# The prompt rows' output projection inside the decode stage, with the difference values loaded and multiplied in two halves

## Chip, cores and metric

One NeuronCore of one Trainium2 chip. The metric is the device time of one execution in microseconds (us), lower is better. The engines are TensorE (PE in the profile; PEld is its weight load), VectorE (DVE), ScalarE (ACT), GpSimd (POOL) and SyncE (SP), which issues most DMAs.

## What is computed

One decoder layer, for 512 prompt tokens and for 8 sequences of 4 new tokens each (32 decode tokens) that attend to a paged cache of 1024 tokens. What matters here:

```python
o = sigmoid(ga) * o_a + sigmoid(gb) * o_b      # o_a: sparse (NSA) attention, o_b: difference attention
h = x + o @ w_o                                # the output projection, w_o is 1024 x 1024
hn = rmsnorm(h, mlp_g)
y = h + square(relu(hn @ w_up)) @ w_down       # D_FF = 4096
```

All inputs are fp32. For the decode tokens `o_a` needs scores against selected pages, a window and compressed keys of the cache, and `o_b` needs `a @ v` with `a = softmax(s1) - lam * softmax(s2)` over all 8 pages of 128 cached keys of each sequence.

## The kernel before, in words

The stages follow one another: projection and compression, prompt attention (`prompt_attention`), decode attention (`decode_attention`, 847 to 1118 us of the profile), and `finish` (from 1118 us), with the output projection, the norm and the MLP.

**Decode stage.** The 8 sequences are treated in four pairs. `decode_steps` writes the order out by hand: a list of steps, 55 for pair 0 and 57 for each later one. A step is a block that PE turns (`turn`, transposes or products into one bank of `ps_t`, g % 4), that ACT or DVE copies into `slot` (owner by parity, with exceptions), and that PE then multiplies (`multiply`). PE's loop goes by two steps: turn g and g+1, then multiply g-2 and g-1. The kinds are: `cmp`, `sel_n`, `win_n`, `sel` (8), `win` (4), `dif_n` (4), `dif` (8 key pages by 4), the value steps `p_sel`, `p_few`, `p_win`, and `p_dif`, `p_dif_n`, which multiply the difference probabilities of pair i with the value pages `dv`; they stand after the sixth `sel` step of pair i+1. `dif` 0 and 1 stand ahead of the value steps, `dif` 2 to 7 behind them.

SP issues the page loads in a written order with waits in between: `load_v(pages, i, k)` brings value page k of both sequences into `dv[:, b, k]` (2 x 512 KB; for i > 0 it waits until `p_dif` of the pair before has read the place, semaphore `dv_read`), `load_k` key page k into one of four places (waits `turned`), `sel_load` and `win_load` the pages of the next pair (behind `nsa_mm`, the end of `p_win`). In pairs 0 to 2 the order is: six value pages, key 4, value 6, key 5, value 7, [wait `nsa_mm`], sel 0-2, key 6, sel 3-5, key 7, sel 6-7, windows, keys 0-3 of the next pair. At the end `closing_loads` (L314) brings half of `w_o` and the prompt's `o` rows for `finish`.

**Finish.** `w_o` (4 MB) and the turned `o` rows are split into a high and a low fp32r part (`wo_high`, `wo_low`, `high_parts`, `low_parts`), and `project_rows(t, half)` (L3194 to L3196) makes each of the 8 tiles of 128 rows by 512 columns as 3 x 8 fp32r matmuls. DVE adds `x` (`add`, L3000), ACT and DVE norm the rows (`root`, `inverse_root`, `norm`), PE turns them (L3182), and they are split again for the MLP. The 32 decode rows go their own way: the last pair's difference output is finished and stored (`end_difference`, `store_difference`), read back with the gates (L2861), merged (`merge_samples`), turned, projected with plain fp32 (`project_samples`, L3206), added, normed and turned. The first up-product (`up`, L3231 to L3233) has two halves of tokens: 0 to 271 and 272 to 543. The second one needs row tile 3 and the decode rows. SP loads MLP weight pieces only after `project_samples`.

Of the kernel before, what the change touches and what calls it, by code (L numbers as in the profile page):

```python
# [51 lines left out]
QT = SEQ // P  # L52
TT = QT + 1
# [7 lines left out]
class Chain:  # L61
# [18 lines left out]
    "pg_copied", "imp_mm", "imp_read", "nsa_mm", "diff_mm", "nsa_read", "diff_read", "o_sq", "o_root", "nsa_out",  # L80
    "diff_out", "nsa_stored", "diff_stored", "sel_read", "dve_step")
FI_SEMS = ("consts_in", "h_in0", "h_in1", "h_in2", "h_in3", "h_in4", "sample_in0", "sample_in1", "w_in0", "w_in1",
    "wo_hi", "wo_lo", "w_hi", "w_split", "merged", "normed", "turned", "t_hi", "t_lo", "o_done", "up_done",
# [54 lines left out]
class Shared:  # L138


    def __init__(self, nc, ctx):
# [21 lines left out]
        self.o_in, self.wo_in = [s.sem(f"o_in{t}") for t in range(QT)], [s.sem(f"wo_in{k}") for k in range(3)]  # L163
# [149 lines left out]

def closing_loads(sp, d, g):  # L314

    sp.dma_start(g.big[:, 0, :].rearrange("p (k c) -> p k c", k=KT),
                 d["w_o"].rearrange("(k p) n -> p k n", p=P)[:, :, 0:CW]).then_inc(g.wo_in[0], 16)
    for t in range(QT):
        sp.dma_start(prompt_rows(g)[:, t, :], d["oa"][P * t:P * (t + 1), :]).then_inc(g.o_in[t], 16)
# [1764 lines left out]
DIFF_STEPS = (("p_dif", 0, 0), ("p_dif_n", 0, 0))  # L2084
KEYS_FIRST = 2


def decode_steps():

    out = []  # L2090
    for i in range(PAIRS):
        key_steps = lambda a, b: [(i, "dif", k, m) for k in range(a, b) for m in range(4)]
        out += [(i, *x) for x in CMP_STEPS]
        out += [(i, "sel", k, 0) for k in range(6)]
        if i:
            out += [(i - 1, *x) for x in DIFF_STEPS]
# [3 lines left out]
        first = KEYS_FIRST if i + 1 < PAIRS else N_PAGES  # L2100
        out += key_steps(0, first) + [(i, *x) for x in VALUE_STEPS] + key_steps(first, N_PAGES)
    return out + [(PAIRS - 1, *x) for x in DIFF_STEPS]

# [15 lines left out]
def decode_attention(nc, d, shared, held, next_held):  # L2119


    with ExitStack() as ctx:
# [7 lines left out]
        dv = s.sb("dv", [P, 2, N_PAGES, DHEADS * DV])  # L2130
        FEW_ROWS, KEY_ROWS, VALUE_ROWS = (slice(x, x + DEC_T) for x in (0, 32, 64))
# [23 lines left out]
        ps_t = s.ps("ps_t", [P, 4, CW])  # L2155
# [17 lines left out]
        nsa_mm, diff_mm, nsa_read, diff_read = s.sem("nsa_mm"), s.sem("diff_mm"), s.sem("nsa_read"), s.sem("diff_read")  # L2173
        o_sq, o_root, nsa_out, diff_out = s.sem("o_sq"), s.sem("o_root"), s.sem("nsa_out"), s.sem("diff_out")
        nsa_stored, diff_stored, sel_read = s.sem("nsa_stored"), s.sem("diff_stored"), s.sem("sel_read")
        step_sem = s.sem("dve_step")
        block = ctx.enter_context(nc.Block())
# [33 lines left out]
        DIFF_AT = {AT[i, "p_dif_n", 0, 0] + (16 if i + 1 < PAIRS else 4): i for i in pairs}  # L2211
# [16 lines left out]
        def pieces(g):  # L2228
# [4 lines left out]
            if kind == "cmp":  # L2233
                return [(slice(0, P), slice(0, 2 * P))]
            if kind == "p_few":
                return [(FEW_ROWS, slice(0, 2 * P)), (slice(0, ROWS), slice(4 * ROWS, 5 * ROWS)),
                        (slice(ROWS, P), slice(5 * ROWS, 6 * ROWS))]
# [5 lines left out]
        def _(sp):  # L2243
# [16 lines left out]
            def load_dv_new(i):  # L2260
                if i:
                    sp.wait_ge(diff_mm, i)
# [3 lines left out]
            def load_v(pages, i, k):  # L2266
                if i:
                    sp.wait_ge(dv_read, N_PAGES * (i - 1) + k + 1)
                for b in range(2):
                    sp.dma_start(dv[:, b, k, :], d["cache_diff"][bass.ds(pages[b][k], 1), :, 1024:2048]  # L2270
                                 .rearrange("n p e -> (n p) e")).then_inc(dv_in[k], 16)
# [16 lines left out]
            for i in range(PAIRS - 1):  # L2288
# [6 lines left out]
                for k in range(6):  # L2295
                    load_v(pages, i, k)
                load_k(pages, i, 4)
                load_v(pages, i, 6)
                load_k(pages, i, 5)
                load_v(pages, i, 7)  # L2300
# [10 lines left out]
                for k in range(KEY_PAGES):  # L2311
                    load_k(following, i + 1, k)
# [11 lines left out]
            sp.wait_ge(sel_read, 1)  # L2324
            closing_loads(sp, d, shared)

        @block.gpsimd
        def _(pool):
            for i in pairs:
                at = 2 * DEC_T * i + SEQ  # L2330
                pool.wait_ge(nsa_out, i + 1)
                for b in range(2):
                    pool.dma_start(d["oa"][at + DEC_T * b:at + DEC_T * (b + 1), :].rearrange("t (h e) -> h t e", e=DK),
                                   o_n[ROWS * b:ROWS * (b + 1), :]).then_inc(nsa_stored, 16)
                if i + 1 < PAIRS:
                    pool.wait_ge(diff_out, i + 1)
                    for b in range(2):
                        store_difference(pool, d, o_d, i, b, diff_stored)
# [4 lines left out]
        def _(pe):  # L2343
# [4 lines left out]
            def turn(g):  # L2348
                i, kind, k, m = STEPS[g]
                bank = ps_t[:, g % 4, :]  # L2350
# [45 lines left out]
                elif kind == "p_dif":  # L2396
                    pe.wait_ge(coef_ready, 5 * i + 5)
                    for x in range(N_PAGES):
                        ins = pe.matmul(bank[:, 64 * x:64 * (x + 1)], s_dif[:, P * x:P * (x + 1)], cd[:], start=True, stop=True)
# [4 lines left out]
            def multiply(g):  # L2404
# [64 lines left out]
                elif kind == "p_dif":  # L2469
                    if i:  # L2470
                        pe.wait_ge(diff_read, i)
                    for x in range(N_PAGES):
                        pe.wait_ge(dv_in[x], 32 * i + 32)
                        for b in range(2):
                            for half in range(2):
                                o = 64 * b + 32 * half
                                ins = pe.matmul(ps_d[o:o + 32, :], tile[:, 64 * x + 32 * b:64 * x + 32 * b + 32],
                                                dv[:, b, x, CW * half:CW * (half + 1)], start=x == 0, stop=False)
                        ins.then_inc(dv_read, 1)
                else:  # L2480
                    pe.wait_ge(dv_n_in, 16 * i + 16)
                    stand()
                    for b in range(2):
                        for half in range(2):
                            o = 64 * b + 32 * half
                            ins = pe.matmul(ps_d[o:o + 32, :], tile[VALUE_ROWS, 32 * b:32 * b + 32],
                                            dv_n[:, b, CW * half:CW * (half + 1)], start=False, stop=True)
                    ins.then_inc(diff_mm, 1)
# [30 lines left out]

            for g in range(0, N + 2, 2):  # L2520
# [6 lines left out]
                for x in (g, g + 1):  # L2527
# [4 lines left out]
                    if x in Q_STEP:  # L2532
                        turn_queries(Q_STEP[x])

        @block.scalar
        def _(act):
            def exp(i, kind, tile, n):
# [4 lines left out]
            for g in range(TAIL):  # L2542
                if g < N and owner[g] == "act":
                    act.wait_ge(turned, g + 1)
                    for rows, cols in pieces(g):
                        ins = nc.scalar.activation(slot[rows, g % 4, cols], ps_t[rows, g % 4, cols], ACT.Copy)  # L2546
                    ins.then_inc(copied["act"], 1)
                if g in EXP_DIF:
# [12 lines left out]
        def _(dve):  # L2561
# [90 lines left out]
            for g in range(TAIL):  # L2652
                if g < N and owner[g] == "dve":
                    dve.wait_ge(turned, g + 1)
                    for rows, cols in pieces(g):
                        ins = nc.vector.tensor_copy(slot[rows, g % 4, cols], ps_t[rows, g % 4, cols])  # L2656
                    ins.then_inc(copied["dve"], 1)
                if g in READ_AT:
# [60 lines left out]
                if g in DIFF_AT:  # L2719
                    i = DIFF_AT[g]  # L2720
                    dve.wait_ge(diff_mm, i + 1)
# [20 lines left out]
HALF = D_FF // 2  # L2742
FT = HALF // P
WS = 2048
PAIR = TOKENS // 2


def finish(nc, d, shared, held):

    with ExitStack() as ctx:  # L2750
# [6 lines left out]
        o_samples = s.over("o_samples", [P, KT, N_DEC], fh_at + 8 * KT * CW, F32)  # L2757
        fl = s.sb("fl", [P, FT, TOKENS], F32R)
        yt = s.sb("yt", [P, KT, TOKENS])
# [3 lines left out]
        o_rows = prompt_rows(shared)  # L2763

        wo_raw = [x.rearrange("p (k c) -> p k c", k=KT) for x in
                  (shared.big[:, 0, :], yt[:].rearrange("p a c -> p (a c)")[:, 0:KT * CW])]
        wo_h, wo_l = (x[:].rearrange("p a c -> p (a c)")[:, 0:2 * KT * CW].rearrange("p (h k c) -> p h k c", h=2, k=KT)
                      for x in (fh, fl))
        more = [shared.big[N_DEC * k:N_DEC * (k + 1), 1, 2 * D_MODEL:].rearrange("p (j c) -> p j c", j=4) for k in range(2)]
        squares = shared.big[:, 1, 0:D_MODEL]  # L2770
        normed = [shared.big[:, 1, D_MODEL + CW * x:D_MODEL + CW * (x + 1)] for x in range(2)]
# [3 lines left out]
        gain = shared.late  # L2775
# [8 lines left out]
        o_in, wo_in = shared.o_in, shared.wo_in  # L2784
        sample_in = [s.sem(f"sample_in{k}") for k in range(2)]
        w_in = [s.sem(f"w_in{k}") for k in range(2)]
        wo_hi, wo_lo, w_hi, w_split = s.sem("wo_hi"), s.sem("wo_lo"), s.sem("w_hi"), s.sem("w_split")
# [12 lines left out]
        NU = HALF // 256  # L2800
        w_o = d["w_o"].rearrange("(k p) n -> p k n", p=P)
        w_up = d["w_up"].rearrange("(k p) n -> p k n", p=P)
        w_down = d["w_down"].rearrange("(k p) n -> p k n", p=P)

        def piece(n):

            half, c = divmod(n, 2 * NU)
            if c < NU:
                return w_up[:, :, HALF * half + 256 * c:HALF * half + 256 * (c + 1)], KT
            return w_down[:, FT * half:FT * (half + 1), P * (c - NU):P * (c - NU + 1)], FT  # L2810

# [3 lines left out]
        TURNS = [(what, t, k) for what, t in (("o", 0), ("o", 1), ("o", 2), ("o", 3), ("h", 0), ("o", QT), ("h", 1), ("h", 2),  # L2815
                                              ("h", QT), ("h", 3)) for k in range(2)]
        TURN = {x: r for r, x in enumerate(TURNS)}
        NORMS = [0, 1, 2, QT, 3]
        PRODUCTS = [(0, 0), (1, 0), (0, 1), (1, 1), (2, 0), (2, 1), (QT, 1), (3, 0), (3, 1)]
        PRODUCT = {x: r for r, x in enumerate(PRODUCTS)}  # L2820
        bank_of = lambda t, half: 2 * (t % 3) + half
        STRIPS = [(q // 4, 2 * (q % 4)) for q in range(8)]

        def wo_strip(x, q):
# [575 lines left out]
```

## Time and profile before

| | us |
|---|---|
| median of 3 runs | 1582.24 |
| lowest, highest | 1574.03, 1583.41 |
| span of the profiled execution (first to last instruction) | 1579.5 |
| decode stage, first key loads to the start of finish | 849.98 to 1118.11 |
| finish, start to the first up-product | 1118.11 to 1178.70 |
| finish, start to the second half of tokens | 1118.11 to 1187.55 |

The profiled execution's own device time is not printed apart from its span; the median of the runs lies 2.7 us above that span. A row of the timeline gives start, duration, engine, line, operation, output and inputs, and in brackets the idle time just before it with what ended it. Times of PE overlap by a modelled drain, so the distance between two starts is what an operation costs. An fp32 product has two records for each matmul of the program; a transpose and an fp32r product have one.

### The profile page before, as it was taken

The page shows a single profiled execution, that of the slowest core. Times are in us where ns is not written, and L with a number is a line of the kernel's source. Part 1 is how long each engine was busy: PE and PEld are TensorE (multiplying, and loading weights), DVE is VectorE, ACT ScalarE, POOL GpSimd, SP SyncE. Part 2 cuts the span into 40 slices and gives each one's busy share as a digit, 9 for nine tenths or more (in the row PEclk, how much of TensorE's full clock was granted, in tenths as well). Part 3 has the DMA queues.
Part 4 walks back from the last instruction along what each step waited for, and adds up shares of the span by engine and source line. Part 5 has one row for each costly group of instructions (what it writes and reads, how often), then busy time and mean ns, then how long its engine had stood idle before and what let it go on. Part 6 is the DMA issues. An engine that isn't in the chain of part 4 may idle for free. (4 is left out here: it accounts for less than half of the span.)

```text
span 1579.5 us, 31804 instructions
## 1 busy us (share of the span) xinstructions
PE 1504.6 (95%) x12648; PEld 1259.9 (80%) x12648; DVE 845.3 (54%) x1823; ACT 603.4 (38%) x1171; POOL 184.1 (12%) x269
## 2 busy tenths in 40 slices
PE   7999999999999989898988899999999999999998
PEld 5778888777899967665656666757689999999998
DVE  4866541323899849876775354535464432244322
ACT  5323211223555548676673233324333321133210
POOL 1001000000545000174421000000000000000000
PEclk9999999999999989999998999989899999999999
DMA  7635368554434176335325999997533344334221
GB/s 207 194 140 170 129 235 314 182 132 115 119 101 125 37 219 186 93 116 137 103 74 175 386 378 369 350 356 257 197 92 107 118 122 124 115 115 123 80 80 57
DMA packets 186010, 265.79 MB, mean 168 GB/s; under 512 B 36381, under 2 KB 117725, under 8 KB 185766
## 3 DMA queue, kind: packets, MB, share of 16 engines
q1 hardware_dynamic: 174930, 227.27, 44.2%
q0 software_dynamic: 6016, 25.34, 5.4%
q10 hardware_dynamic: 4948, 11.62, 2.0%
q8 instruction: 74, 1.21, 0.3%
q14 instruction: 42, 0.34, 0.1%
HBM read 241.11 MB, written 42.60 MB: 180 GB/s over the span
## 5 line engine op out<-in xcount | busy, mean ns | idle before, releaser
L779 PE MATMUL pj_ps<-all_hi,pj_xh 128*128 128x512 f32 x480 | 192.1, 400 | 0.3 <-DVE all_lo L651 0.3
L781 PE MATMUL pj_ps<-all_hi,pj_xl 128*128 128x512 f32 x480 | 189.9, 396 | 0.0
L780 PE MATMUL pj_ps<-all_lo,pj_xh 128*128 128x512 f32 x480 | 189.8, 395 | 0.0
L3231 PE MATMUL fi_ps<-fi_th,fi_wh 128*128 128x272 f32 x512 | 147.6, 288 | 1.7 <-DVE fi_tl L2988 1.7
L3232 PE MATMUL fi_ps<-fi_fl,fi_wh 128*128 128x272 f32 x512 | 148.5, 290 | 0.0
L3233 PE MATMUL fi_ps<-fi_th,fi_wl 128*128 128x272 f32 x512 | 148.3, 290 | 0.0
L3231 PE MATMUL fi_ps<-fi_fh,fi_wh 128*128 128x272 f32 x512 | 147.8, 289 | 0.0
L3233 PE MATMUL fi_ps<-fi_fh,fi_wl 128*128 128x272 f32 x512 | 147.6, 288 | 0.0
L3232 PE MATMUL fi_ps<-fi_tl,fi_wh 128*128 128x272 f32 x512 | 147.2, 287 | 0.0
L2546 ACT ACTIVATE de_slot<-de_ps_t 128x512 f32<-128x512 f32 (+5 forms) x124 | 62.8, 513 | 171.0 <-PE de_ps_t L2380 87.7
L2656 DVE COPY de_slot<-de_ps_t 128x512 f32<-128x512 f32 (+4 forms) x112 | 68.8, 623 | 105.9 <-PE de_ps_t L2380 61.0
L325 POOL DMA_INDIRECT all_first<-in_cache_nsa,all_row_ids x64 | 73.5, 1148 | 406.8 <-PE pj_ps L787 219.6
L1806 ACT ACTIVATE pa_sc<-pa_sc,pa_nmax 128x128 f32<-128x128 f32 (+3 forms) x192 | 105.8, 557 | 14.3 <-DVE pa_nmax L1933 14.0
L779 PEld LDWEIGHTS pj_ps<-all_hi,pj_xh 128*128 128x128 f32 x480 | 90.1, 188 | 25.3 <-issue 4.3
L2903 ACT ACTIVATE fi_wh<-all_big 128x2048 fp32r<-128x2048 f32 x30 | 57.3, 1909 | 138.5 <-PE fi_ps L3233 138.5
L781 PEld LDWEIGHTS pj_ps<-all_hi,pj_xl 128*128 128x128 f32 x480 | 90.2, 188 | 21.9
L780 PEld LDWEIGHTS pj_ps<-all_lo,pj_xh 128*128 128x128 f32 x480 | 90.2, 188 | 20.8
L3231 PEld LDWEIGHTS fi_ps<-fi_th,fi_wh 128*128 128x128 f32 x512 | 96.4, 188 | 1.9 <-issue 1.9
L3231 PEld LDWEIGHTS fi_ps<-fi_fh,fi_wh 128*128 128x128 f32 x512 | 96.5, 189 | 0.0
L3232 PEld LDWEIGHTS fi_ps<-fi_tl,fi_wh 128*128 128x128 f32 x512 | 96.5, 188 | 0.0
L3233 PEld LDWEIGHTS fi_ps<-fi_fh,fi_wl 128*128 128x128 f32 x512 | 96.4, 188 | 0.0
L3233 PEld LDWEIGHTS fi_ps<-fi_th,fi_wl 128*128 128x128 f32 x512 | 96.2, 188 | 0.0
(414 smaller groups left out, 3307.7 us busy)
## 6 DMA issues: line engine op xcount, KB each, us to landing
de_dv<-in_cache_diff SPq DMA_DIRECT2D x64, 512.0 KB, 10.1
all_big<-in_w_in SPq DMA_DIRECT2D x14, 2048.0 KB, 10.6
de_dk<-in_cache_diff SPq DMA_DIRECT2D x48, 512.0 KB, 9.4
all_big<-in_cache_nsa SPq DMA_DIRECT2D x64, 256.0 KB, 6.0
all_big<-in_w_up SPq DMA_DIRECT2D x16, 1024.0 KB, 5.5
all_big<-in_w_down SPq DMA_DIRECT2D x16, 1024.0 KB, 5.6
all_dk<-in_cache_diff SPq DMA_DIRECT2D x16, 512.0 KB, 8.0
all_win<-in_cache_win SPq DMA_DIRECT2D x32, 256.0 KB, 7.1
```

The costliest lines, as they stand in the source:

```text
L325: nc.gpsimd.indirect_dma_start(dst[:, 4 * block + s, :], None, rows, bass.IndirectOffsetOnAxis(ap=g.row_ids[:, 4 * pair + block, s:s + 1], ...
L779: pe.matmul(ps[:, t, :], xh[:, k, xk], wh[:, u, k, :], start=k == 0, stop=False)
L780: pe.matmul(ps[:, t, :], xh[:, k, xk], wl[:, u, k, :], start=False, stop=False)
L781: return pe.matmul(ps[:, t, :], xl[:, k, xk], wh[:, u, k, :], start=False, stop=k == KT - 1)
L1806: nc.scalar.activation(tile, tile, ACT.Exp, scale=-1.0, bias=nmax[:, x.n % 6, a:a + 1], accum_out=x.sums[a]).then_inc(probs, 1)
L2546: ins = nc.scalar.activation(slot[rows, g % 4, cols], ps_t[rows, g % 4, cols], ACT.Copy)
L2656: ins = nc.vector.tensor_copy(slot[rows, g % 4, cols], ps_t[rows, g % 4, cols])
L2903: nc.scalar.activation(wh[:, u, :], w[:, u, :], ACT.Copy).then_inc(w_hi, 1)
L3231: pe.matmul(o, hi[:, k, :], a_hi[:, k, tok], start=k == 0, stop=False)
L3232: pe.matmul(o, hi[:, k, :], a_lo[:, k, tok], start=False, stop=False)
L3233: return pe.matmul(o, lo[:, k, :], a_hi[:, k, tok], start=False, stop=k == n_k - 1)
```

## The change

Four parts.

1. *The prompt's projection moves into the decode stage.* Beside steps 10 to 24 of pair 0, PE turns the `o` rows, eight pieces of 128 x 512 (`turn_rows`), each loaded by ACT's DMA queue into one of two places of `side`, and copied by ACT. Then `project_rows(n, part)` makes 8 products of 128 x 512, each in four parts of two plain fp32 matmuls, one part to each turn of PE's loop: products 0 to 3 from step 26 to step 56, products 4 to 7 from step 68 to step 98. DVE adds `x`, POOL loads `x` and stores `h` into the scratch `q`.
2. *Room for it.* The half of `w_o` and the turned rows lie in value places 4 to 7 of `dv`. So pair 0's eight value pages share places 0 to 3: pages 4 to 7 are loaded after `p_dif` has read 0 to 3, and pair 1's pages 4 to 7 wait for all eight products. `p_dif` has two steps of four pages, in all pairs. `ps_t` has three banks instead of four, the fourth is `ps_w`.
3. *SP's order.* Pair 0: values 0-3, keys 4, 5, ..., keys 0, 1 of pair 1, values 4-7 of pair 0, keys 2, 3. Pair 1: keys 4, 5, values 0-3, then values 4-7 behind the wait for the eighth product, and behind them everything else of that pair. Pairs 2 and 3 are as before.
4. *Finish.* The fp32r split of `w_o`, the turning of the `o` rows and the 8 products are gone. `h` is loaded from scratch, the first two MLP pieces are loaded at the end of the decode stage, `w_o` is loaded once more by POOL for the decode rows. Those are turned and projected after the first half of the up-product.

The core of the diff:

```diff
-DIFF_STEPS = (("p_dif", 0, 0), ("p_dif_n", 0, 0))
+DIFF_STEPS = (("p_dif", 0, 0), ("p_dif_n", 0, 0), ("p_dif", 1, 0))
+RING_PAGES = 4
...
+            out += [(i - 1, *x) for x in (DIFF_STEPS[:2] if i == 1 else DIFF_STEPS)]
...
+            out += key_steps(0, KEYS_FIRST)
+            if i == 1:
+                out += [(0, *x) for x in DIFF_STEPS[2:]]
...
+SIDE_TURNS, SIDE_ROWS = 2 * QT, 2 * QT
+SIDE_FIRST, SIDE_PARTS, SIDE_PAUSE = 5, KT // 2, 5
+def side_turn_at(j):
+    return 2 * (SIDE_FIRST + j)
+def side_part_at(n, part):
+    return 2 * (SIDE_FIRST + SIDE_TURNS + SIDE_PARTS * n + part + (SIDE_PAUSE if n >= QT else 0))
...
             def load_v(pages, i, k):
+                if i == 1 and k >= RING_PAGES:
+                    sp.wait_ge(proj_mm, SIDE_ROWS)
+                elif i == 0 and k >= RING_PAGES:
+                    sp.wait_ge(dv_read, k - RING_PAGES + 1)
+                elif i == 1:
+                    sp.wait_ge(dv_read, RING_PAGES + k + 1)
...
+                elif i == 1:
+                    for k in (4, 5):
+                        load_k(pages, i, k)
+                    for k in range(N_PAGES):
+                        load_v(pages, i, k)
...
             def turn(g):
+                bank = ps_t[:, g % 3, :]
+                if g >= 3 and g % 2:
+                    pe.wait_ge(copied[owner[g - 3]], level[g - 3])
+                    stand()
...
+            def turn_rows(j):
+                pe.wait_ge(side_in[j % 2], 16 * (j // 2) + 16)
+                if j:
+                    stand()
+                    pe.wait_ge(o_copied, j)
+                for k in range(4):
+                    ins = pe.transpose(ps_w[:, P * k:P * (k + 1)], side[:, j % 2, P * k:P * (k + 1)], ident[:])
+                ins.then_inc(o_turned, 1)
+            def project_rows(n, part):
+                if part == 0:
+                    pe.wait_ge(wo_in, 16 * (n // QT + 1))
+                    stand()
+                    if n:
+                        pe.wait_ge(proj_added, n)
+                    else:
+                        pe.wait_ge(o_copied, SIDE_TURNS)
+                for k in (2 * part, 2 * part + 1):
+                    ins = pe.matmul(ps_w[:], o_t[:, k, tile_of(n)], half_wo[:, k, :], start=k == 0, stop=k == KT - 1)
+                if part == SIDE_PARTS - 1:
+                    ins.then_inc(proj_mm, 1)
...
+            def copy_o(j):
+                act.wait_ge(o_turned, j + 1)
+                nc.scalar.activation(o_t[:, 4 * c:4 * c + 4, P * t:P * (t + 1)], ps_w[:]..., ACT.Copy).then_inc(o_copied, 1)
+                if j + 2 < SIDE_TURNS:
+                    load_o(j + 2)
...
+                if g in ADD_H:
+                    dve.wait_ge(proj_mm, n + 1)
+                    dve.wait_ge(x_in[n % 2], 16 * (n // 2 + 1))
+                    nc.vector.tensor_tensor(side[:, n % 2, :], ps_w[:], side[:, n % 2, :], ALU.add).then_inc(proj_added, 1)
```

and of `finish`, PE's order (the fp32r form of `project_rows` is deleted):

```diff
-            turn("o", 0)
-            turn("o", 1)
-            project_rows(0, 0)
...
-            turn("h", QT)
+            for t in range(3):
+                turn("h", t)
             pe.wait_ge(w_split, 1)
             pe.wait_ge(t_lo, TURN["h", 2, 1] + 1)
-            pe.wait_ge(h_added, PRODUCT[3, 0] + 1)
             up(0, 0, 0)
+            turn("h", 3)
             up(0, 1, 0)
-            turn("h", 3)
-            pe.wait_ge(h_added, PRODUCT[3, 1] + 1)
+            turn("o", QT)
+            project_samples()
+            turn("h", QT)
             pe.wait_ge(t_lo, len(TURNS))
             up(0, 0, 1).then_inc(up_done, 1)
```

## Rows read from the trace of the kernel before

**Rows 1.** Busy time by window, all engines: pairs 0 to 3, stage, finish's start, MLP
```profile
core 0: us, PE busy (x) PEld busy (x) DVE busy (x) ACT busy (x) POOL busy (x), PEclk, DMA share, GB/s
850.00:909.80 59.80, 54.57 (x795) 42.56 (x794) 28.08 (x82) 17.10 (x35) 1.15 (x2) 0.88 1.02 371
...
973.30:1041.60 68.30, 63.61 (x893) 45.43 (x890) 31.18 (x88) 21.10 (x41) 3.32 (x6) 0.93 0.99 366
...
850.00:1118.10 268.10, 251.00 (x3558) 180.11 (x3556) 122.41 (x344) 84.40 (x165) 11.10 (x20) 0.93 0.94 343
1118.10:1187.60 69.50, 65.66 (x385) 53.76 (x385) 44.93 (x66) 29.09 (x47) 3.05 (x2) 0.95 0.39 131
```
**Rows 2.** What PE waited for in the decode stage (total, times, longest)
```profile
PE de_ps_t L2380 <- DMA de_dk<-in_cache_diff: 10.3, 5, 3.6
```
**Rows 3.** Timeline of PE: undisturbed turns of its loop, and one difference value step
```profile
953.26 1.09 PE L2380 MATMUL de_ps_t<-all_ident,de_dk 128*128 128x128 f32 x8
954.29 0.64 PE L2437 MATMUL de_ps_s<-de_slot,de_qdb 128*32 128x128 f32 x16
954.86 1.09 PE L2380 MATMUL de_ps_t<-all_ident,all_dk 128*128 128x128 f32 x8
...
958.06 1.09 PE L2380 MATMUL de_ps_t<-all_ident,de_dk 128*128 128x128 f32 x8
...
1052.44 7.07 PE L2477 MATMUL de_ps_d<-de_dv,de_slot 128*32 128x512 f32 x64
```
**Rows 4.** Timeline of PE: key pages 6 and 7 late in pair 0, page 7 in pair 1
```profile
895.36 0.66 PE L2380 MATMUL de_ps_t<-all_ident,de_dk 128*128 128x128 f32 x4
899.65 1.11 PE L2380 MATMUL de_ps_t<-all_ident,de_dk 128*128 128x128 f32 x4 [3.64 <-DMA de_dk<-in_cache_diff]
...
906.66 0.66 PE L2380 MATMUL de_ps_t<-all_ident,de_dk 128*128 128x128 f32 x4 [1.30 <-DMA de_dk<-in_cache_diff]
...
970.09 1.09 PE L2380 MATMUL de_ps_t<-all_ident,de_dk 128*128 128x128 f32 x8 [2.09 <-DMA de_dk<-in_cache_diff]
```
**Rows 5.** Timeline of SP: its DMA issues behind the end of p_win, pair 0
```profile
888.09 0.90 SPq L306 DMA_DIRECT2D de_dk<-in_cache_diff  x2
889.20 3.05 SPq L289 DMA_DIRECT2D all_big<-in_cache_nsa  x6
892.29 0.88 SPq L2253 DMA_DIRECT2D de_vc<-scratch_vc_s  x1
893.22 2.83 SPq L2257 DMA_DIRECT2D de_gates<-scratch_g  x2
896.24 1.36 SPq L306 DMA_DIRECT2D de_dk<-in_cache_diff  x2
```
**Rows 6.** DMA issues of the decode stage, 850 to 1125: number, KB each, us to landing
```profile
de_dv<-in_cache_diff SPq DMA_DIRECT2D x64, 512.0 KB, 10.1
...
scratch_oa<-de_o_n POOLq DMA_DIRECT2D x8, 16.0 KB, 4.6
```
**Rows 7.** Timeline of DVE and ACT in finish, the operations that the new start keeps
```profile
1126.31 1.05 DVE L3016 TENSOR_REDUCE all_late<-all_late 128x128 f32<-128x512 f32 x1
...
1143.56 1.29 DVE L2988 TENSOR_TENSOR fi_tl<-fi_ps,fi_th 128x512 fp32r<-128x512 f32 x2 [0.38 <-ACT fi_th L2909]
...
1145.60 1.41 DVE L3037 SCALAR_TENSOR_TENSOR all_big<-fi_h,fi_rstd,all_late 128x512 f32<-128x512 f32 x2
...
1175.53 2.27 DVE L3043 TENSOR_TENSOR fi_wl<-all_big,fi_wh 128x2048 fp32r<-128x2048 f32 x1
```
**Rows 8.** Timeline in finish: an fp32r product's matmul, the second half of tokens
```profile
1166.21 0.40 PE L3195 MATMUL fi_ps<-fi_fl,fi_th 128*128 128x512 f32 x1
1166.44 0.39 PE L3196 MATMUL fi_ps<-fi_fh,fi_tl 128*128 128x512 f32 x1
...
1187.55 0.36 PE L3231 MATMUL fi_ps<-fi_th,fi_wh 128*128 128x272 f32 x1 [1.66 <-DVE fi_tl L2988]
```
**Rows 9.** The chain that ended last, in order of time: the decode rows' projection
```profile
1162.35 3.59 PE fi_ps L3206 x64
```

More of the change, by code:

```diff
@@ L2130, in decode_attention @@
         dv = s.sb("dv", [P, 2, N_PAGES, DHEADS * DV])
+        side = s.sb("side", [P, 2, CW])
+        half_wo, o_t = (dv[:, x, RING_PAGES:, :].rearrange("p a c -> p (a c)").rearrange("p (k c) -> p k c", k=KT) for x in range(2))
         FEW_ROWS, KEY_ROWS, VALUE_ROWS = (slice(x, x + DEC_T) for x in (0, 32, 64))
@@ L2210, in decode_attention, with value_place @@
         QB_AT = after(Q_STEP, 1)
-        DIFF_AT = {AT[i, "p_dif_n", 0, 0] + (16 if i + 1 < PAIRS else 4): i for i in pairs}
+        DIFF_AT = {AT[i, "p_dif", 1, 0] + (16 if i + 1 < PAIRS else 4): i for i in pairs}
+        TURN_O = {side_turn_at(j): j for j in range(SIDE_TURNS)}
+        COPY_O = after(TURN_O, 2)
+        PROJ = {side_part_at(n, part): (n, part) for n in range(SIDE_ROWS) for part in range(SIDE_PARTS)}
+        ADD_H = {side_part_at(n, SIDE_PARTS - 1) + 3: n for n in range(SIDE_ROWS)}
+        STORE_H = after(ADD_H, 3)
+        half_of = lambda n: slice(CW * (n // QT), CW * (n // QT + 1))
+        tile_of = lambda n: slice(P * (n % QT), P * (n % QT + 1))
+        def value_place(i, k):
+            if i == 0:
+                return k % RING_PAGES, 32 * (k // RING_PAGES + 1)
+            return k, 32 * (i + 2) if k < RING_PAGES else 32 * i
         ROOT_AT, DIFF_END = after(DIFF_AT, 2), after(DIFF_AT, 4)
@@ L2311, in _ @@
                 for k in range(KEY_PAGES):
+                    if i == 0 and k == KEYS_FIRST:
+                        for v in range(RING_PAGES, N_PAGES):
+                            load_v(pages, i, v)
                     load_k(following, i + 1, k)
@@ L2324, in _ @@
             sp.wait_ge(sel_read, 1)
+            for u in range(2):
+                sp.wait_ge(h_stored[u], 16 * (SIDE_ROWS // 2))
             closing_loads(sp, d, shared)
@@ L2396, in turn @@
                 elif kind == "p_dif":
-                    pe.wait_ge(coef_ready, 5 * i + 5)
-                    for x in range(N_PAGES):
-                        ins = pe.matmul(bank[:, 64 * x:64 * (x + 1)], s_dif[:, P * x:P * (x + 1)], cd[:], start=True, stop=True)
+                    if k == 0:
+                        pe.wait_ge(coef_ready, 5 * i + 5)
+                    for x in range(4):
+                        page = 4 * k + x
+                        ins = pe.matmul(bank[:, 64 * x:64 * (x + 1)], s_dif[:, P * page:P * (page + 1)], cd[:], start=True, stop=True)
                 else:
@@ L2469, in multiply @@
                 elif kind == "p_dif":
-                    if i:
+                    if i and k == 0:
                         pe.wait_ge(diff_read, i)
-                    for x in range(N_PAGES):
-                        pe.wait_ge(dv_in[x], 32 * i + 32)
+                    for x in range(4):
+                        place, arrived = value_place(i, 4 * k + x)
+                        pe.wait_ge(dv_in[place], arrived)
                         for b in range(2):
@@ L2762, in finish @@
         wl = s.sb("wl", [P, 2, WS], F32R)
[L2763 to L2771, printed above, removed]
+        rows_h = prompt_rows(shared)
+        more = [gated[N_DEC * k:N_DEC * (k + 1), :, :] for k in range(2)]
+        normed = [norm_rows[:, x, :] for x in range(2)]
         relu = shared.big[:, 1, 0:TOKENS]
@@ L2877, in _ @@
         def _(pool):
+            for half in range(2):
+                pool.dma_start(wo[:, half, :, :], w_o[:, :, CW * half:CW * (half + 1)]).then_inc(wo_in[half], 16)
             for k in range(2):
```

368 lines of the change are left out of this document (171 added, 197 removed).

## The prediction, made before the changed kernel ran

> **What bounds the kernel now.** I read the span's windows first, then PE's waits and the timeline of PE and SP in the decode stage, then the start of finish. In the decode stage PE is busy for 251.0 of 268.1 us and the DMA engines for 94% of the time; the first three pairs run at 99% DMA share or more [rows 1]. So this stage has two limits close together, and neither has much room. In finish, PE is busy for 65.66 of the first 69.50 us while the DMA share is 0.39 [rows 1]: there the projection's matmuls set the time. PE's only large wait in the decode stage is for key pages, 10.3 us in five waits [rows 2]. Undisturbed, PE's loop turns and multiplies two steps in 1.60 us (953.26 to 954.86) [rows 3].
>
> **The change, step by step.** The sum is made against the profiled span of 1579.5 us; the median of the runs is 2.7 us above it.
>
> *(a) What the products cost PE in the decode stage.* The trace has no plain fp32 product of full width. The nearest row is the difference value step: 64 records of 512 columns, four at a time in four column groups of the array, take 7.07 us, so 16 passes in series at 0.442 us [rows 3]. A product of full width can't share the array and has two passes for each matmul. 64 matmuls x 2 x 0.442 = 56.6 us. Lower bound: the fp32r matmul of the same width starts every 0.23 us (1166.21 to 1166.44) [rows 8], and if each pass took only that, 64 x 2 x 0.23 = 29.4 us. Upper bound: the record's own length as if nothing overlapped, about 0.6 us a pass, 77 us. I take 56.6, since that row has the same type and the same number of columns. Turning the `o` rows: 32 transposes. A turn of the loop holds 8 of them and has 1.03 us from its start to the multiplication (953.26 to 954.29) [rows 3], so 32 x 0.13 = 4 us. Each of the 32 parts also breaks the chain of matmuls; the loop has about 1.60 - 1.03 - 0.4 = 0.2 us of gaps already, and I add 0.1 us for each, 3 us (0 to 6).
>
> *(b) The new waits around them.* A product's first part waits for DVE to have added the product before. DVE comes to that addition only behind the copy of step g+3, which PE turns in the very loop turn at whose end the next product stands: turn about 0.9 us, copy and addition 0.7 us each, against 1.6 us until PE is there. That is 0.9 us for six products (not for the first nor for the one behind the pause): 5.4 us (0 to 8). The `o` rows have two places. Load j+2 is issued after copy j, and PE wants it about 4 us after turn j (two loop turns of 1.6 and two turnings). From turn to copy is 1.7 us; the load lies beside the key and value pages. A DMA on another queue than SP's lands in 4.6 us there, one on SP's in 10.1 [rows 6]. With 4.6, three rounds lose 1.7 + 4.6 - 4.1 = 2.2 us each, 7 us with the first load behind the 2 MB of `w_o`. Bounds: 0 if it lands within 2.4 us, and 7 + 3 x 5.5 = 24 us at 10.1. I take 7, by the row of the other queue.
>
> *(c) What the stage gives back in pairs 0 and 1.* Key pages 6 and 7 of pair 0 are late now: from the turn at 895.36 to the one at 906.66 PE does two and a quarter loop turns, 3.7 us of work, in 11.3 us; of the rest 4.9 us are the two waits and 2.7 us a lower clock behind them [rows 4]. With some 14 us of products in between and four value pages fewer ahead, those keys will be there: 7.6 us saved. So the end of the last part, which falls at 957.5 in today's time (behind the turns that start before 958.06 [rows 3], half a loop turn earlier), comes at 957.5 - 7.6 + 56.6 + 4 + 3 + 5.4 + 7 = 1025.9.
>
> *(d) The queue behind the eighth product.* This is the step that I weigh most. In pair 1 SP now waits for all eight products before value pages 4 to 7, and the selected pages of pair 2 and key pages 6 and 7 of pair 1 stand behind it. PE needs key page 6 only three loop turns later, at 1025.9 + 4.8. In front of it go 4 x 2 x 512 KB of values, 6 x 256 KB of selected pages and its own 1024 KB, 6.8 MB. At the 371 GB/s of pair 0 [rows 1] that is 18.3 us, and about 1 us until the first bytes move: 19.4. Page 7 follows after three more issues and 2.6 MB, 7.0 us, just as its two landings are apart in pair 0 (899.65 and 906.66 [rows 4]; SP's issues of them are 8.2 us apart [rows 5]). So PE goes on with page 7 at 1025.9 + 26.4 = 1052.3. Today it does so at 970.09 [rows 4]. Shift: +82.2 us. SP's issues, the buffers and the backlog behind this point are the same as now, so the remaining 148 us of the stage keep their length, but for the split `p_dif` (a step more in two pairs, with waits on three banks): +1.5 us.
>
> *(e) Finish.* Gone are 192 fp32r matmuls of 0.23 us [rows 8], 44 us of PE, and the splits beside them. What is left is a chain. ACT: square and root, with a table load, until about 3 us after the start. DVE: the difference sum (1.05 us and three small ones), then for each row tile norm 1.41 and low part 1.29, and the split 2.27 [rows 7]: about 15 us until PE can start the first half. The decode rows end later (times after the start of finish, my estimates from how long the same operations take in it today): difference out at 5.5, stored and read back at 14 to 16, merged at 19.4, low parts and the second split of DVE until 23, turned and copied 23.3, projected (3.59 us [rows 9]) 27, added 29, root 30.7, two norms 32.3, turned and split 34. After such idling PE's clock falls (0.88 to 0.93 in windows with waits [rows 1]), so I add 2: the second half starts 36 us after the start instead of 1187.55 - 1118.1 = 69.4 [rows 1, 8]. Gain: 33.4 us (28 to 41). MLP loads ahead cost nothing there, the DMA share is 0.39.
>
> *Sum.* 1579.5 + 82.2 + 1.5 - 33.4 = 1629.8 of span, and with the 2.7 us to the median 1632.5, **1633 us**. In short: 60 us of PE work go into a stage that has 17 us of idle PE, about 45 us leave a stage where they were the limit but a chain of 36 us stays, and a new wait stands in front of late key pages.
>
> *The page that bears on (b).* The Trainium skill, page "DMA: Bandwidth & Descriptors", section "Queues, rings and completion order", says that each DMA engine goes round between the queues that have work, a packet at a time. By that rule ACT's small loads don't stand behind SP's backlog, which agrees with the 4.6 us of the other queue [rows 6]. Were it otherwise the third rival below would hold.
>
> **The rivals.**
>
> *Light side work.* The gaps, the additions and the `o` loads all hide (DVE and ACT are busy for less than half of the stage [rows 1]). Then 3 + 5.4 + 7 = 15.4 us go: 1617 us. Against it: PE's loop is written in order and each of the waits stands in its path.
>
> *Late side loads.* The `o` loads land like SP's own at 10.1 us [rows 6]: +17 us, 1650 us. For it: all 16 DMA engines are full in pair 0 [rows 1]. Against it: the other queue's 4.6 us.
>
> *The other side: transfers pace the stage, and the products fill PE's holes.* For it: DMA share 0.99 and more in pairs 0 to 2 [rows 1]. The holes are PE's idle 17.1 us and the time lost at a lower clock, 7% of 268.1 = 18.8 us [rows 1], 36 us together. It decides from the point where the holes take in over 56.6 + 4 + 1.5 - 33.4 = 29 us of the products, with no new wait for keys. With all 36: 1582.2 - 7 = 1575 us, and with finish at its best bound (41 us) 1568. Against it: most holes lie in pairs 2 and 3 or at the ends, where no product is put, and 957.5 to 1118 isn't touched by the products at all; in pairs 0 and 1 I find only the 7.6 us of (c) and the 2.1 us of page 7 in pair 1 [rows 4].
>
> **How the numbers follow.** Forecast 0.52, light side work 0.18, late side loads 0.20, the other side 0.08, others 0.02. A measurement of this kernel can tell about 1% from no change. The other side is split between faster by over 1% (under 1566 us) and within 1%: faster 0.04, same 0.05, slower 0.91. The range: below, light side work and the better bound of finish, 1617 less the 8 us that finish's better bound adds, and 5 for keys that land faster, 1604; above, late loads with the upper bounds of the gaps (3) and of finish (5), 1658.
>
> **What would show it.** Right: some 128 records of the new products about 0.44 us apart, 57 us of PE; PE waits of 12 to 17 us for key page 6 of pair 1 and 1 to 4 us for page 7; finish's second half of tokens about 36 us behind its start; the stage longer by about 85 us, with a lower DMA share in pairs 0 and 1. Wrong: passes of clearly under 0.4 us, no key wait behind the eighth product, or a stage that is longer by less than 45 us. If the `o` turns stand 4 us or more apart from each other the side loads are late.

## The result, and the profile after

| | before | after |
|---|---|---|
| median, us | 1578.7 (4 runs beside it; 1579.1 over all 17) | 1645.7 (1642.5 to 1650.3) |
| ratio | | 1.041, 95% interval 1.038 to 1.044 (the two medians alone give 1.042) |
| span of the profiled execution | 1579.5 | 1648.6 |
| start of decode stage (DVE clears `qb`) | 848.0 | 852.0 |
| start of finish (DVE sets `eps`) | 1118.2 | 1217.75 |
| decode stage, one to the other | 270.2 | 365.7 |
| finish, start to second half of tokens | 69.4 | 36.7 |

The change made the kernel 4% slower. The decode stage is 95.5 us longer, and finish reaches the second half of tokens 32.7 us sooner after its start. 4.0 us of the profiled difference lie ahead of the decode stage; over the twelve profiles of this case that start lies anywhere between 846.5 and 854.2 us, so I read nothing into it. The lengths between the two marks leave it out, and I compare stages by them. One run of short_products, of 2950.5 us, was disturbed and is left out below.

The busy time by window of the changed kernel, columns as in [rows 1]; the windows are the stretch of the products with the last turnings of the `o` rows (890 to 1036), the time behind them in which PE stands (1045 to 1061), and then the stage and the start of finish:

```profile
890.00:1036.00 146.00, 140.08 (x1383) 85.40 (x1383) 42.74 (x117) 26.86 (x52) 10.39 (x19) 0.98 0.62 220
```
```profile
1045.00:1050.00 5.00, 0.00 (x0) 0.00 (x0) 0.00 (x0) 0.00 (x0) 0.63 (x2) 0.50 1.03 411
1050.00:1055.00 5.00, 0.00 (x0) 0.00 (x0) 0.00 (x0) 0.00 (x0) 0.00 (x0) 0.50 1.03 327
1055.00:1061.00 6.00, 0.00 (x0) 0.00 (x0) 0.00 (x0) 0.00 (x0) 0.00 (x0) 0.50 1.04 316
```
```profile
850.00:1217.70 367.70, 313.61 (x3744) 208.76 (x3744) 129.40 (x360) 88.29 (x172) 20.77 (x38) 0.92 0.78 279
1217.70:1254.50 36.80, 20.57 (x161) 17.27 (x161) 25.53 (x42) 17.53 (x31) 5.38 (x4) 0.70 0.76 262
```

Against [rows 1] the stage's PE busy time grows from 251.0 to 313.6 us, and the DMA share falls from 0.94 to 0.78. While the products run, PE is the full engine (140 of 146 us) and the DMA engines are at 0.62. Soon behind them, from 1045 to 1061, it is the other way round: the DMA share is over 1, PE does nothing and its granted clock is 0.50, the lower of its two levels, 1.2 GHz. Two limits that were side by side before now take turns. What PE waited for between 845 and 1230 us, four lines of the view (compare [rows 2]):

```profile
PE de_ps_t L2483 <- DMA de_dk<-in_cache_diff: 26.6, 3, 19.8
PE de_ps_w L2633 <- DMA de_side<-scratch_oa: 10.0, 4, 4.8
PE fi_ps L3269 <- DVE fi_norm_rows L3144: 7.4, 1, 7.4
PE de_ps_w L2645 <- DVE de_side L2822: 5.5, 6, 1.3
```

L2633 is the turning of the `o` rows, L2645 the products. The timeline of PE around them (form of [rows 3, 4]):

```profile
865.61 0.43 PE L2618 MATMUL de_ps_n<-de_gm,de_s_cmp 128*64 128x128 f32 x2
870.86 1.12 PE L2633 MATMUL de_ps_w<-all_ident,de_side 128*128 128x128 f32 x4 [4.82 <-DMA de_side<-scratch_oa]
...
879.43 0.63 PE L2633 MATMUL de_ps_w<-all_ident,de_side 128*128 128x128 f32 x4 [2.66 <-DMA de_side<-scratch_oa]
...
897.57 1.98 PE L2645 MATMUL de_ps_w<-de_dv 128*128 128x512 f32 x4
899.39 1.05 PE L2491 MATMUL de_ps_t<-de_cm,de_s_sel 128*128 128x128 f32 x8
...
915.91 1.99 PE L2645 MATMUL de_ps_w<-de_dv 128*128 128x512 f32 x4 [0.88 <-DVE de_side L2822]
```
```profile
1034.03 1.98 PE L2645 MATMUL de_ps_w<-de_dv 128*128 128x512 f32 x4
1035.85 0.60 PE L2483 MATMUL de_ps_t<-all_ident,all_dk 128*128 128x128 f32 x4
...
1040.92 0.67 PE L2483 MATMUL de_ps_t<-all_ident,de_dk 128*128 128x128 f32 x4
1061.42 1.11 PE L2483 MATMUL de_ps_t<-all_ident,de_dk 128*128 128x128 f32 x4 [19.83 <-DMA de_dk<-in_cache_diff]
...
1068.50 0.93 PE L2483 MATMUL de_ps_t<-all_ident,de_dk 128*128 128x128 f32 x4 [1.89 <-DMA de_dk<-in_cache_diff]
```

A part, two plain fp32 matmuls of full width, takes 1.82 us (897.57 to 899.39), four passes of 0.455. One of the 32 parts ran at the lower clock. The last part ends at 1035.85; PE goes on with key page 6 at 1061.42 and with page 7 at 1068.50. SP's issues say why (form of [rows 5]), with the line of SP's own waits between 845 and 1100 us ahead of them:

```profile
SPq L2339 <- PE de_ps_w L2645: 24.2, 1, 24.2
```
```profile
1036.18 4.34 SPq L2339 DMA_DIRECT2D de_dv<-in_cache_diff  x8
...
1041.47 4.29 SPq L295 DMA_DIRECT2D all_big<-in_cache_nsa  x6
...
1047.76 1.02 SPq L312 DMA_DIRECT2D de_dk<-in_cache_diff  x2
1048.98 4.86 SPq L295 DMA_DIRECT2D all_big<-in_cache_nsa  x6
...
1058.24 0.95 SPq L312 DMA_DIRECT2D de_dk<-in_cache_diff  x2
```

SP has issued value pages 0 to 3 by 1011.8 and then stands for 24.2 us at the wait for the eighth product (L2645). Four value pages and three selected pages, each for two sequences, stand ahead of key page 6, all issued only when that product is done. In finish, PE's first turning waits 7.4 us for the first normed rows, and the decode rows come last:

```profile
1222.40 1.97 PE L3269 MATMUL fi_ps<-all_ident,fi_norm_rows 128*128 128x128 f32 x8 [7.38 <-DVE fi_norm_rows L3144]
...
1244.52 3.66 PE L3278 MATMUL fi_ps<-fi_wo,fi_o_samples 128*32 128x256 f32 x64 [0.61 <-DVEq L3110]
1252.48 0.43 PE L3269 MATMUL fi_ps<-all_ident,fi_norm_rows 32*128 32x32 f32 x4 [4.30 <-DVE fi_norm_rows L3144]
```

The second half of tokens starts at 1254.46, with PE at the lower clock: its granted clock is 0.55 over the next 6 us, where the kernel before has 1.00.

### The profile page after: what moved, and what is told of

Same layout as the page of the kernel before. It is cut to its first block and busy times, and to the rows that moved or that the text cites. A ratio compares the mean times of both kernels' runs of the same rounds, so it can differ in the third digit from the quotient of the medians.

```text
span 1648.6 us, 31808 instructions
## 1 busy us (share of the span) xinstructions
PE 1528.9 (93%) x12584; PEld 1257.7 (76%) x12584; DVE 834.8 (51%) x1812; ACT 596.4 (36%) x1162; POOL 193.8 (12%) x287
## 5 line engine op out<-in xcount | busy, mean ns | idle before, releaser
L2815 DVE COPY de_slot<-de_ps_t 128x512 f32<-128x512 f32 (+5 forms) x117 | 69.6, 602 | 199.5 <-PE de_ps_t L2483 128.3
L2700 ACT ACTIVATE de_slot<-de_ps_t 128x512 f32<-128x512 f32 (+3 forms) x123 | 63.1, 517 | 265.1 <-PE de_ps_t L2483 147.7
```

## The experiments

The theory: the products' PE time is added to a stage with little idle PE, and the loads that wait behind the eighth product hold up the keys. The rivals: the bytes set the pace whatever their order; the small waits around the side work make the difference; making room for the work costs by itself. All ratios are to the kernel before.

**keys_first.** One part of SP's order in pair 1 is turned:

```diff
                 elif i == 1:
                     for k in (4, 5):
                         load_k(pages, i, k)
-                    for k in range(N_PAGES):
+                    for k in range(RING_PAGES):
                         load_v(pages, i, k)
...
                 load_k(pages, i, 7)
+                if i == 1:
+                    for k in range(RING_PAGES, N_PAGES):
+                        load_v(pages, i, k)
```

> The changed kernel, with SP's order in pair 1 turned: key pages 6 and 7 and the selected pages 0 to 5 are issued ahead of the value pages 4 to 7, and so ahead of the wait for the eighth product. Theory (the new wait stands in front of the key loads): PE's waits for keys behind the eighth product (19.8 and 1.9 us in the changed kernel) go, with the low clock behind them, and the time falls by 20 to 25 us, to about 1622 us. Rival (after the eighth product the transfers set the pace, 11.5 MB of them, whatever their order): the wait moves to the values or to the keys of pair 2 and the time falls by less than 8 us.

Measured: 1624.5 us, ratio 1.027 (1.024 to 1.031), 21 us less than the changed kernel; the stage is 341.6 us long, 24 less. PE's waits behind the eighth product, the first lines of the view for 1020 to 1110:

```profile
PE de_ps_t L2486 <- DMA de_dk<-in_cache_diff: 3.2, 1, 3.2
PE de_ps_s L2545 <- DVE de_slot L2818: 1.4, 2, 0.9
```

The two key waits of pair 1 are gone and nothing of their size came in their place: the 3.2 us belong to a key page of pair 2, for which PE waits 4.87 us in the changed kernel. The order set the wait, not the bytes.

**add_early, o_first.** DVE's addition two steps earlier, and the `o` rows ahead of `w_o` in ACT's queue:

```diff
-        ADD_H = {side_part_at(n, SIDE_PARTS - 1) + 3: n for n in range(SIDE_ROWS)}
+        ADD_H = {side_part_at(n, SIDE_PARTS - 1) + 1: n for n in range(SIDE_ROWS)}
```
```diff
-            load_half(0)
             for j in range(2):
                 load_o(j)
+            load_half(0)
```

> The changed kernel, with DVE's addition of a product two steps earlier in its list (at step g+1 instead of g+3), so that it doesn't stand behind the copy of a step that PE has yet to turn. Theory: PE's six waits for the addition (5.5 us in all) fall to under 1 us and the time by about 5 us, since all of them lie ahead of the eighth product, on whose end the key loads hang. Rival (PE's waits there are covered): under 2 us.

> The changed kernel, with the first two loads of o rows ahead of the half of w_o in ACT's queue. Theory (side loads wait for their own queue, the 2 MB ahead of them): PE's first wait of 4.8 us for the o rows goes and the first turns come 5 us earlier; the later rounds (1.2 to 2.7 us each) stay, since their loads are issued only behind a copy; the time falls by 4 to 5 us. Rival (they wait for SP's backlog on the shared DMA engines): the first wait stays over 3 us and the time within 2 us.

Measured: add_early 1641.6 us (ratio 1.038, 1.035 to 1.042), o_first 1643.0 us (1.038, 1.035 to 1.041). In add_early the waits of the products for DVE are no longer among PE's waits, and the stage is 358.5 us long, 7 less; the median moved by 4 us, as expected in size, though this is near what a measurement can tell. In o_first the stage keeps its length (366.9 against 365.7 us) and the median is 2.7 us lower, between theory and rival. Its turnings of the `o` rows:

```profile
869.17 0.66 PE L2633 MATMUL de_ps_w<-all_ident,de_side 128*128 128x128 f32 x4
...
871.53 0.66 PE L2633 MATMUL de_ps_w<-all_ident,de_side 128*128 128x128 f32 x4
...
878.78 1.09 PE L2633 MATMUL de_ps_w<-all_ident,de_side 128*128 128x128 f32 x4 [5.25 <-DMA de_side<-scratch_oa]
```

The first wait is gone, as the theory has it. The two first pieces are issued beside SP's six key pages in both kernels and land in 6.0 and 7.5 us here, against 16.8 and 17.5 us behind the `w_o` half in the changed kernel. But PE now waits 5.25 us for the third piece, where it waited 2.66. That piece is issued while the `w_o` half is still under way (issued at 856.50, landed 20.9 us later); it takes 8.3 us instead of 6.4. So part of the wait moved by two pieces, and my 4 to 5 us did not come. In the changed kernel the three pieces issued next, when the half had landed, took 6.4, 6.3 and 6.0 us beside a full SP queue, in which the value pages issued between 850 and 880 us took 14.4 (median). The Trainium skill, page "DMA: Bandwidth & Descriptors", section "Queues, rings and completion order", says that each DMA engine goes round between the queues that have work for it, and that it takes up the descriptors of one queue in their order, though they need not finish in it. These landing times agree with both: beside the other queue a piece is slowed but does not stand behind its backlog, behind 2 MB of its own queue it does.

**three_mends.** The three edits together.

> The three edits of keys_first, add_early and o_first in one kernel. Theory: they add up, 30 to 35 us less than the changed kernel, about 1613 us, and still 30 us or more above the kernel before, because the products' own 58 us of PE and the turns stay in a stage that gives back only some 10 us, while finish gives back 33. Rival (the waits alone made the change slow): it comes to 1585 us or less.

Measured: 1617.0 us, ratio 1.023 (1.019 to 1.027), the stage 336.7 us. So 29 us of the 67 go with the waits, just under the 30 to 35 expected, and 38 stay. Waits of 7.9 us for the `o` rows and 3.5 us for a key page are still among them. The changed kernel isn't slow by its waits alone.

**short_products.** 48 of the 64 matmuls are not issued, so this kernel leaves out most of the projection:

```diff
-                for k in (2 * part, 2 * part + 1):
+                for k in {0: (0,), SIDE_PARTS - 1: (KT - 1,)}.get(part, ()):
```

> The changed kernel with 2 of the 8 matmuls of each product (the first and the last); the other 48 matmuls are left out, and all waits, loads, turns and additions stay. Theory (PE's own time sets pairs 0 and 1): 48 x 0.91 = 44 us less, about 1602 us, with the wait for key page 6 as long as before (about 20 us), since it starts from the eighth product's end. Rival (transfers pace the stage and the products fill holes): under 15 us less.

Measured: three runs of 1603.8, 1605.7 and 1612.9 us, ratio on record 1.019 (1.014 to 1.025), 33 to 42 us less than the changed kernel; in its profile the stage is 324.0 us long, 41.7 less. The wait for key page 6 is there as before:

```profile
1016.30 1.11 PE L2483 MATMUL de_ps_t<-all_ident,de_dk 128*128 128x128 f32 x4 [19.15 <-DMA de_dk<-in_cache_diff]
```

The stage gives back 0.87 us for each matmul left out, against 0.91 in the timeline. Nearly every microsecond of these 48 matmuls was added to the stage; the picture of products in PE's holes falls.

**no_side, no_side_late.** No side work at all, and the prompt's projection is left out; no_side drops the wait ahead of value pages 4 to 7 of pair 1, in no_side_late they wait for a step instead of the product (cut to the two main edits):

```diff
-        PROJ = {side_part_at(n, part): (n, part) for n in range(SIDE_ROWS) for part in range(SIDE_PARTS)}
+        PROJ = {}
...
                 if i == 1 and k >= RING_PAGES:
-                    sp.wait_ge(proj_mm, SIDE_ROWS)
+                    sp.wait_ge(turned, 100)
```

> The changed kernel without any side work in the decode stage: no o rows turned, no products, no additions, no loads and stores for them, and the value pages 4 to 7 of pair 1 not waited for; finish then reads whatever lies in its scratch rows, and the prompt's projection is left out. The four value places of pair 0, the three banks and the split p_dif stay. It shows what making room costs and what finish gives. Theory: the kernel before less 32.5 us in finish, and 1.5 for the extra steps, and up to 10 us because 4 MB of pair 0's values are loaded later in a stage whose DMA engines are full: 1548 to 1560 us. Rival (making room is itself a main cost): 1570 us or more.

> no_side, but value pages 4 to 7 of pair 1 wait until PE has turned step 99, where the eighth product would end. No product is in it. Theory (the place of the wait costs, not the products): PE waits about 20 us for key page 6 of pair 1, and the time is 15 to 25 us above no_side. Rival (the wait is long only because the products and their stores fill the queues): under 5 us above no_side.

Measured: no_side 1567.0 us (0.992, 0.989 to 0.995), no_side_late 1569.4 us (0.994, 0.991 to 0.996); stages 285.2 and 286.5 us. Both of my figures missed: no_side lies between its two expectations, no_side_late inside its rival's (2.4 us above no_side). Making room costs 15.0 us of stage (285.2 against 270.2), where I had expected up to 11.5. The late wait moves key page 6 back by 5.6 us, counted from the stage's start, and PE waits 15.6 us for it instead of 12.1, but the stage is only 1.3 us longer. It isn't the changed kernel's wait, though: SP stands at it for 10.2 us, and in the changed kernel for 24.2. There seven parts of the products and a wait for DVE lie between pair 0's second value step and the end of the eighth product, 30 us in all, and only some 16 us lie between that step and step 99 here. So the run shows that this small delay is nearly absorbed, not that one of 24 us would be.

The timelines of no_side show what happens:

```profile
942.74 12.01 SPq L2339 DMA_DIRECT2D de_dv<-in_cache_diff  x16
...
955.37 7.54 SPq L295 DMA_DIRECT2D all_big<-in_cache_nsa  x6
...
964.80 1.18 SPq L312 DMA_DIRECT2D de_dk<-in_cache_diff  x2
```
```profile
978.01 1.12 PE L2481 MATMUL de_ps_t<-all_ident,de_dk 128*128 128x128 f32 x4 [12.14 <-DMA de_dk<-in_cache_diff]
```

All sixteen value loads of pair 1 come late even with no product in sight: places 0 to 3 are free only after the second half of pair 0's value step, which stands in the middle of pair 1, and the keys stand behind all of them. The wait for the eighth product is one way to be late; sharing four places is another, and in no_side it makes PE wait 12.1 us. In the changed kernel the first way decides: value pages 0 to 3 are issued there by 1011.8, 24 us before the eighth product lets SP go on.

**no_side_keys_first.** no_side with the edit of keys_first; it leaves out the projection as well.

> no_side with SP's order of keys_first: key pages 6 and 7 of pair 1 ahead of the value pages 4 to 7. The prompt's projection is left out as in no_side. Theory (most of what making room costs is the order: the values of pair 1 wait for the late second half of pair 0's value step, and the keys stand behind them; PE waits 12.1 us for key page 6 in no_side): that wait falls to under 2 us and the time by 10 to 13 us, from 1567 to about 1555 us. Rival (making room costs transfers that come later in any order): under 4 us.

Measured: 1561.0 us (0.989, 0.986 to 0.993), 6 us less than no_side, between the two expectations; its runs spread from 1553.8 to 1567.6. The wait for key page 6 falls from 12.1 to 2.5 us. The profiled stage is 276.3 us, 9 less than no_side's, but that profile is of the fastest of the six runs. So the order is some 6 to 9 of the 15 us and the rest of making room stays. No run takes the rest apart into the three banks, the split value step and the later values. Part of the wait only moved: PE's key waits still add up to 15.0 us, against 17.9 in no_side, and the longest is now one of 6.1 us in pair 2:

```profile
PE de_ps_t L2484 <- DMA de_dk<-in_cache_diff: 15.0, 6, 6.1
```

**before_keys_early.** The runs point at the keys' place in SP's order, so I tried it on the kernel before:

```diff
                 sp.wait_ge(nsa_mm, i + 1)
-                sel_load(sp, d, shared, following, range(0, 3))
+                load_k(pages, i, 6)
+                sel_load(sp, d, shared, following, range(0, 2))
+                load_k(pages, i, 7)
+                sel_load(sp, d, shared, following, range(2, 6))
                 load_new(i + 1)
-                load_k(pages, i, 6)
-                sel_load(sp, d, shared, following, range(3, 6))
                 load_new_v(i + 1)
-                load_k(pages, i, 7)
```

> The kernel before with one edit in SP's order in pairs 0 to 2: behind the end of p_win key page 6 first, then the selected pages 0 and 1, then key page 7, and only then the rest. Theory (PE's key waits of 10.3 us in the kernel before, and the low clock behind them, come from the keys standing behind loads that nobody needs yet): the waits fall to under 4 us and the time by 5 to 10 us, to about 1573 us, faster than both kernels. Rival (the stage is bound by its bytes, 0.99 DMA share): the waits move to other pages and the time stays within 3 us.

Measured: 1568.3 us over 12 runs, ratio 0.994 (0.992 to 0.996): about 10 us faster than the kernel before, the upper end of what the theory gave, and the fastest that computes the whole layer. Its stage is 257.8 us long, and the key waits of [rows 2] are gone from PE's list; a smaller one came, for the new rows, which are now loaded later. The first two lines of that list, between 850 and 1105 us, and the stage's busy times:

```profile
PE de_ps_t L2368 <- DMA de_new_rows<-out_diff_s: 4.3, 3, 2.9
PE de_ps_s L2437 <- DVE de_slot L2656: 2.0, 3, 0.9
```
```profile
850.00:1105.00 255.00, 244.15 (x3552) 177.32 (x3552) 122.57 (x344) 84.59 (x165) 11.11 (x20) 0.95 0.97 360
```

The DMA share went up from 0.94 to 0.97 with the same bytes (343 GB/s over 268.1 us before, 360 over 255.0 here). Counted from the stage's start, PE comes to the difference value steps of pairs 0 to 3 earlier by 4.5, 4.5, 8.4 and 11.3 us. So in the stretches ahead of the first and the third of them the share of 0.99 and more in [rows 1] did not mean that the bytes were the limit. Between the first and the second nothing was gained, and for that stretch the run leaves it open.

**mends_keys_early.** The same order in three_mends.

> three_mends with the same order of keys in all three pairs. In pairs 0 and 1 the products cover the keys already; it can help only at key pages 6 and 7 of pair 2 (one wait of 3.5 us in three_mends). Theory: 3 to 5 us less than three_mends, about 1613 us. Rival: no difference beyond 2 us.

Measured: 1613.5 us (1.022, 1.018 to 1.025), 3.5 us less than three_mends, as expected in size, but with four runs each that overlap (1612.7 to 1614.9 and 1613.5 to 1621.7) this isn't clear of the noise. The key wait is gone, and one of 2.2 us for the new rows came.

## Why the prediction was right, and where its sizes were off

Direction, place and the main mechanism came out as forecast; the median is 13 us above the 1633 and inside the range. The profiled span shows the error without the scatter of the medians: 1648.6 against 1629.8, 18.8 us more. 11.8 of them are the stage (95.5 us longer, forecast 82.2 + 1.5), 0.7 finish, 2.2 the start of the MLP, and 4.0 the scatter ahead of the stage. That the median looks closer is chance: the changed kernel's profile fell on the slowest of its four runs. By the steps:

- *(a) The products.* 31 parts at 1.82 us and one of 3.5 are 60 us, against 56.6 + 3. The column-grouped value step was the right row to read the pass from. short_products shows for 48 of the 64 matmuls that this time goes into the stage almost whole.
- *(b) The new waits.* The additions cost 5.5 us, as forecast (5.4). The `o` rows are one of the two terms that were mis-sized. From the end of the loop turn with step 10 to the start of the one with step 28 the kernel before takes 12.8 us (862.22 to 875.01 in its timeline), the changed one 31.7 (865.9 to 899.39, less the first part of a product, 1.8). That is 18.9 us for the turnings, where I had 4 + 7. 10.0 of them are waits and 4 the transposes. The step had given the first load 0.4 us for standing behind `w_o`, and that wait alone was 4.8; the rounds behind it lost 5.2 us together, where it had 6.6. The rest, about 5 us, fits the lower clock behind the waits, which the step had left out: eight transposes take 1.91 us there against 1.09, and the granted clock is 0.61 from 880 to 893. The row of 4.6 us that the step went by is of small stores of 16 KB; the loads of 256 KB took 2.9 to 6.4 us once `w_o` was in. (The prediction's paragraph on the page speaks of the "third rival"; it means late side loads, the second.)
- *(c) What comes back.* The key waits of pair 0 are gone, as forecast. The last part ends at 1035.85; my 1025.9 and the 4.0 us from ahead of the stage give 1029.9, 6 short. The `o` rows alone were 7.9 over, so something of the rest came some 2 us better than forecast; no run says what.
- *(d) The queue behind the eighth product.* The second mis-sized term. Key pages 6 and 7 came 25.6 and 32.7 us behind the end of the last part, not 19.4 and 26.4, and PE's wait for page 6 was 19.8 us, over the 12 to 17 named as a sign. The step let the 6.8 MB move at 371 GB/s from the start. But SP needed 11.6 us to issue up to the key; the windows from 1036 to 1045 show 221 and 264 GB/s, and 316 to 411 come only behind that, so that 1036 to 1061 has 311 on average. keys_first shows that this order costs 21 us. The cause was told rightly for this kernel: SP's list of waits has the 24.2 us at the eighth product. It was not told whole, since no_side shows that the shared places hold the keys back too, 12.1 us of wait, when no product is there. The tail, for which the step had 148 us and 1.5 for the split value step, is 149.2 us long. That the room itself costs 15.0 us of stage without side work was in no term; its largest part, the wait for key page 6, is in the changed kernel the same wait as the one behind the product and isn't added to it.
- *(e) Finish.* 36.7 us to the second half of tokens, against 36.
- What is left is small: from the second half of tokens to the end the changed kernel takes 2.2 us more, and its first 6 us there are at a granted clock of 0.55.

Of the rivals, light side work fell: the 10.0 and 5.5 us of waits stand in PE's path, and add_early takes 7 us off the stage. The other side fell by short_products. Late side loads had the rows' cost too high (28 us against 18.9) and the wrong mechanism: behind `w_o` in their own queue they took 17 us, and without it 6.0 to 7.5 (o_first); the next three took 6.0 to 6.4 beside an SP queue whose value pages took 14.4.

The balance by stage length: making room, measured without side work, 15.0 us; side work with its waits and the longer key wait 80.5 (365.7 against 285.2); finish -32.7. 44 us of matmuls left finish, but the chain through the decode rows kept it from giving back more.

## What to carry to other kernels

Before work is moved into a stage because its transfers bind it, look at the idle time of the engine that has to do the work, in just the stretch where it goes; here both were near full, and the moved work was simply added. If an order of loads is written by hand, put first what is needed first: a load that must wait for a buffer holds everything behind it. Here a DMA share of 0.99 showed that the engines were busy, not that they carried the bytes which were wanted next.

## What the runs showed that I had not expected

- A stage at 0.94 DMA share with PE busy for 94% could still lose 12 us by a new order of the same loads (before_keys_early).
- Waits of 1 to 5 us cost more than their own length: the 10.0 us of waits for the `o` rows came with some 5 us that fit the lower clock behind them.
- With all products and the wait for the eighth left out, but with the shared places kept, PE still waits 12.1 us for key page 6, where the changed kernel has 19.8.
